# Three single-precision-part products in place of fp32 ones in the first mixer's branch and output projections

## What is computed

```python
def hybrid_mixer(x, w_in, b_gate, ..., w_branch_dn, w_branch_sb, w_out):
    proj = x @ w_in
    ...
    gate = jax.nn.sigmoid(gates.reshape(b, l, N_BRANCH, d) + b_gate)
    merged = (gate[:, :, 0] * (o_dn.astype(x.dtype) @ w_branch_dn)
              + gate[:, :, 1] * (o_sb.astype(x.dtype) @ w_branch_sb))
    return merged @ w_out
...
mix = hybrid_mixer(h, ...)
h = layer_norm(DEEPNORM_ALPHA * h + mix, ln1_g[i], ln1_b[i])
ffn = hierarchical_moe(h, ...)      # router, then 32 experts, top 2 of a group
```

## Time and profile before

| | |
|---|---|
| Time before | 1086.28 us, median of 3 runs (1086.09 to 1087.94) |
| Profiled execution | 1088.23 us, of which 1086.1 us lie between its first and last instruction (the span) |
| PE busy | 983.1 us, 91% of the span |
| VectorE, ScalarE, GpSimd busy | 498.5, 354.2 and 33.8 us |
| DMA | 229.38 MB, 211 GB/s over the span |
| Mean granted TensorE clock | 0.964 of 2.4 GHz |

### The profile page before, as it was taken

One profiled execution on the slowest core, in us unless ns is written; L12 is line 12 of the kernel. 1 busy time (PEld: TensorE's weight loads), 2 busy tenths in 40 slices (PEclk: granted clock), 3 DMA queues, 4 the chain that ended last, 5 costly groups with the idle time before them and its releaser, 6 DMA issues.

```text
span 1086.1 us, 14285 instructions
## 1 busy us (share of the span) xinstructions
PE 983.1 (91%) x6105; PEld 726.6 (67%) x6105; DVE 498.5 (46%) x777; ACT 354.2 (33%) x456; POOL 33.8 (3%) x51
## 2 busy tenths in 40 slices
PE   8989989999999984656877999999999989999996
PEld 7988776444456432213336887599998879889995
DVE  5973563271246102001038446355656565655554
ACT  3555303841022110001025436134343334434341
POOL 1400100021000000000000000000000000000000
PEclk9989999999999997878999999999999999999999
DMA  9724420452942999999995460445545344545520
GB/s 334 218 86 148 147 88 1 155 184 97 415 156 100 417 421 421 421 421 421 422 396 189 156 227 5 155 155 191 197 164 222 118 154 155 213 175 198 189 77 39
DMA packets 67126, 229.38 MB, mean 211 GB/s; under 512 B 4080, under 2 KB 5392, under 8 KB 54400
## 3 DMA queue, kind: packets, MB, share of 16 engines
q1 hardware_dynamic: 65216, 223.28, 54.2%
q0 software_dynamic: 1632, 5.26, 1.3%
q10 hardware_dynamic: 224, 0.07, 0.0%
HBM read 227.54 MB, written 1.05 MB: 210 GB/s over the span
## 4 chain that ended last, share of the span: by engine, by line
PE 74%; DMA 12%; DVE 9%; issue 2%; SPq 2%; ACT 1%; DVEq 0%; ACTq 0%
PE bank L1253 17%; PE bank L1264 16%; PE bank L1036 5%; DMA ring<-in_expert_w_up 5%; PE bank L676 4%; DMA arena<-in_expert_w_up 3%; PE bank L1162 3%; PE bank L665 3%; PE bank L960 3%; PE bank L929 3%; PE bank L1229 3%; PE bank L652 2%; DMA arena<-in_expert_w_down 2%; DVE arena L1744 2%; PE bank L1167 2%
## 5 line engine op out<-in xcount | busy, mean ns | idle before, releaser
L2174 DVE TENSOR_TENSOR w_lo<-ring,w_hi 128x2048 fp32r<-128x2048 f32 x76 | 170.6, 2288 | 97.4 <-ACT w_hi L1556 97.4
L1556 ACT ACTIVATE w_hi<-ring 128x2048 fp32r<-128x2048 f32 x76 | 141.1, 1909 | 87.9 <-PE bank L1264 86.9
L1253 PE MATMUL bank<-xT_hi,w_hi 128*128 128x256 f32 x512 | 143.8, 281 | 2.6 <-DVE xT_lo L2162 2.6
L1253 PE MATMUL bank<-xT_hi,w_lo 128*128 128x256 f32 x512 | 143.6, 280 | 0.0
L1253 PE MATMUL bank<-xT_lo,w_hi 128*128 128x256 f32 x512 | 143.2, 280 | 0.0
L1264 PE MATMUL bank<-w_hi,hidden_lo 128*128 128x512 f32 x256 | 99.9, 390 | 0.0
L1264 PE MATMUL bank<-w_lo,hidden_hi 128*128 128x512 f32 x256 | 99.8, 390 | 0.0
L1264 PE MATMUL bank<-w_hi,hidden_hi 128*128 128x512 f32 x256 | 99.6, 389 | 0.0
L1253 PEld LDWEIGHTS bank<-xT_hi,w_hi 128*128 128x128 f32 x512 | 96.1, 188 | 3.5 <-issue 3.0
L1253 PEld LDWEIGHTS bank<-xT_lo,w_hi 128*128 128x128 f32 x512 | 96.4, 188 | 0.5
L1253 PEld LDWEIGHTS bank<-xT_hi,w_lo 128*128 128x128 f32 x512 | 95.9, 187 | 0.0
(11 more groups left out here) (489 smaller groups left out, 1621.5 us busy)
## 6 DMA issues: line engine op xcount, KB each, us to landing
ring<-in_mlp_w_up SPq DMA_DIRECT2D x32, 1024.0 KB, 6.6
ring<-in_mlp_w_down SPq DMA_DIRECT2D x32, 1024.0 KB, 6.3
ring<-in_w_in SPq DMA_DIRECT2D x22, 1024.0 KB, 7.6
ring<-in_expert_w_down SPq DMA_DIRECT2D x22, 1024.0 KB, 19.7
ring<-in_expert_w_gate SPq DMA_DIRECT2D x16, 1024.0 KB, 15.4
ring<-in_expert_w_up SPq DMA_DIRECT2D x16, 1024.0 KB, 17.4
arena<-in_expert_w_gate SPq DMA_DIRECT2D x15, 1024.0 KB, 12.8
arena<-in_expert_w_up SPq DMA_DIRECT2D x15, 1024.0 KB, 14.8
```

Of the source, the lines that this page charges most:

```text
L1253: last = mm(B[4 + (2 * j + pr) % 4][:, cc * SEQ:(cc + 1) * SEQ], w_[:, k * 512 + c * P:k * 512 + (c + 1) * P], x_[:, k, 0:SEQ], start=(k = ...
L1556: act(whi[:, n % 2, half], slot(u)[:, half], ACT.Copy).then_inc(S("split_hi"), 1)
L2174: tt(wlo[:, u % SLOTS, half], slot(u)[:, half], f32(whi[:, n % 2, half]), ALU.subtract).then_inc(S("split_lo"), 1)
```

## The change

The two branch projections and the output projection are each made of three single passes. The four weight units are split by halves of 2048 columns (h = 0 to 7). ScalarE writes the hi part of a half to one of three buffers `mid_hi` (in X2, in `params` columns 2048 to 4095 and in `params` columns 0 to 2047), and VectorE writes the lo part over the half in its ring slot. `mid_split(h)` waits for the half to land and, from h = 3 on, for the products that read the buffer last (`HALF_FREE`). The left operands are split too: `od_hi`, `od_lo`, `os_hi`, `os_lo`, `xT_hi` and `mix_lo`. A bank is summed over both halves of a unit. Since `params` and X2 are in use longer, expert units 0 and 1 now wait for the end of the output projection. The constants `lower_r` and `ones_r` move from X2 to `arena`.

```diff
+    mid_hi = [parts("mid_hi0", "X2", 0, HALF_U), parts("mid_hi1", "params", 2 * D, HALF_U), parts("mid_hi2", "params", 0, HALF_U)]
...
-    FIRST_USE = [0, 5, 6, 7, 8, 2, 1, 3, 4]
+    FIRST_USE = [8, 5, 6, 7, 2, 3, 0, 1, 4]
...
+    HALF_FREE = ("half_used", 1), ("branch", 4), ("half_used", 2), ("branch", 8), ("half_used", 3)
...
-            elif j == 0:
-                sp.wait_ge(S("gate_out"), 8)
-                sp.wait_ge(S("stream_made"), 2)
-            elif j == 1:
-                sp.wait_ge(S("four_psum"), 4)
+            elif j < 2:
+                sp.wait_ge(S("mixed"), 4)
...
+        def branch(u, ready, hi, lo):
+
+            for part in range(2):
+                h = 2 * (u - 11) + part
+                weights_split(h, "split_hi")
+                passes = (hi, mid_hi[h % 3]), (lo, mid_hi[h % 3]), (hi, wlo[:, u % SLOTS, part * HALF_U:(part + 1) * HALF_U])
+                for p_, n in [(p_, n) for p_ in range(3) for n in range(4)] if part == 0 else [(p_, n) for n in range(4) for p_ in range(3)]:
...
+                    for kk in range(2):
+                        last = mm(B[n], x_(2 * part + kk, i), w_[:, kk * D + half * 512:kk * D + (half + 1) * 512], start=(part == 0 and p_ == 0 and kk == 0), stop=(part == 1 and p_ == 2 and kk == 1))
...
+        def mid_split(h):
+
+            u, half = 11 + h // 2, slice((h % 2) * HALF_U, (h % 2 + 1) * HALF_U)
+            landed(sc, u)
+            if h >= 3:
+                sc.wait_ge(S(HALF_FREE[h - 3][0]), HALF_FREE[h - 3][1])
+            act(mid_hi[h % 3], slot(u)[:, half], ACT.Copy).then_inc(S("split_hi"), 1)
...
+        def mid_low(h):
+
+            u, half = 11 + h // 2, slice((h % 2) * HALF_U, (h % 2 + 1) * HALF_U)
+            dve.wait_ge(S("split_hi"), MID0 + h + 1)
+            tt(wlo[:, u % SLOTS, half], slot(u)[:, half], f32(mid_hi[h % 3]), ALU.subtract).then_inc(S("split_lo"), 1)
+
+        for i in range(NT):
+            dve.wait_ge(S("branch_in"), i + 1)
+            tt(odL[:, 4 * i:4 * i + 4, :], cube(B[6 + i], 4), f32(odH[:, :, i * P:(i + 1) * P]), ALU.subtract).then_inc(S("branch_lo"), 1)
+        mid_low(0)
```

More of the change, by code:

```diff
@@ L223, in build @@
     SP0s, SP1s = (cube(SPH[0], 8), cube(SPL[:, 0:2048], 8)), (cube(SPH[1], 8), cube(SPL[:, 2048:3072], 8))
-    lower_r, ones_r = [parts(f"{n}_r", "X2", P * i, P) for i, n in enumerate(("lower", "ones"))]
+    lower_r, ones_r = [parts(f"{n}_r", "arena", 18240 + P * i, P) for i, n in enumerate(("lower", "ones"))]
+    mid_hi = [parts("mid_hi0", "X2", 0, HALF_U), parts("mid_hi1", "params", 2 * D, HALF_U), parts("mid_hi2", "params", 0, HALF_U)]
+    odH, odL = cube(parts("od_hi", "arena", 8 * L, 1024), 4), cube(parts("od_lo", "arena", 12 * L + 8 * L + 1536, 1024), 8)
+    osH, osL = cube(parts("os_hi", "arena", 4 * L, 1024), 4), cube(parts("os_lo", "arena", 12 * L, 1024), 4)
+    mixL = [cube(parts(f"mix_lo{i}", "X1", (2 * i + 1) * D, D), 4) for i in range(2)]
     wr, rbias = cube(arena[:, 18496:18496 + KD * 36], KD), arena[:, 18784:18820]
@@ L916, in _ @@
             last.then_inc(S("later_psum"), 1)
-        def branch(u, src, n, ready):
-            landed(pe, u)
-            pe.wait_ge(S("branch_in"), ready)
-            for i in range(NT):
-                for half in range(2):
-                    if n < 4:
-                        pe.wait_ge(S("later_out"), n + 1)
-                    else:
-                        pe.wait_ge(S("branch_out"), n - 3)
-                    for k in range(4):
-                        last = mm(B[n % 4], src[:, k, i * P:(i + 1) * P], slab(u, k, D)[:, half * 512:(half + 1) * 512], start=(k == 0), stop=(k == 3))
-                    last.then_inc(S("branch"), 1)
-                    n += 1
@@ L934, in _ @@
+        branch(11, 2, lambda k, i: odH[:, k, i * P:(i + 1) * P], lambda k, i: odL[:, 4 * i + k, :])
         pe.wait_ge(S("masked"), 4)
@@ L1916, in _, with gated @@
             tt(ZM[:, hs, :], ZM[:, hs, :], cube(B[(6, 7, 4, 5)[g]][0:META, :], 2), ALU.subtract).then_inc(S("later_out"), 1)
+        mid_low(1)
+        mid_low(2)
         dve.wait_ge(S("gate_sig"), 8)
-        for n in range(8):
+        def gated(n):
             br, i, half = n // 4, (n // 2) % 2, n % 2
@@ L1923, in _ @@
             tt(g_, g_, B[n % 4], ALU.mult).then_inc(S("branch_out"), 1)
+        for n in range(4):
+            gated(n)
+        mid_low(3)
+        for i in range(NT):
+            dve.wait_ge(S("branch_in"), i + 3)
+            tt(osL[:, 2 * i:2 * i + 2, :], cube(B[6 + i], 2), f32(osH[:, 2 * i:2 * i + 2, :]), ALU.subtract).then_inc(S("branch_lo"), 1)
+        mid_low(4)
+        for n in range(4, 8):
+            gated(n)
         for i in range(NT):
@@ L1926, in _ @@
             tt(gates[:, i, 0, :], gates[:, i, 0, :], gates[:, i, 1, :], ALU.add).then_inc(S("merged"), 1)
-        four_copies(0)
+        dve.wait_ge(S("merged"), 2)
+        for b in range(4):
+            dve.wait_ge(S("turned_act"), b + 1)
+            tt(mixL[b // 2][:, 2 * (b % 2):2 * (b % 2) + 2, :], cube(B[4 + b], 2), f32(xTH[:, 2 * b:2 * b + 2, 0:SEQ]), ALU.subtract).then_inc(S("turned_dve"), 1)
+        for h in range(5, MID):
+            mid_low(h)
         dve.wait_ge(S("stream_made"), 2)
```

79 lines of the change are left out of this document (60 added, 19 removed).

## The result

| | before | after |
|---|---|---|
| Median on one chip, in turns | 1088.12 us (1086.09 to 1089.28, 8 runs) | 1078.20 us (1077.27 to 1083.48, 8 runs) |
| Ratio | | 0.9922, 95% interval 0.9905 to 0.9939 |
| Profiled execution | 1088.23 us, span 1086.1 | 1078.01 us, span 1076.0 |

The change is faster by 8.5 us by the ratio (10.3 to 6.6) and by 9.9 us by the two medians. The ratio is the smaller one since two of the eight executions of after lie well above the rest (1081.62 and 1083.48 us); the means are 8.6 us apart. The sum said 10.3, the two profiled executions are 10.2 apart (spans 10.1).

The account below looks back on a forecast made before the run. PE was taken to bound the kernel (busy 983.1 of 1086.1 us), with the projections all on the path. Gains of 11.0 us less a 0.7 us wait gave -10.3 us: median 1076.0, own range 1074.0 to 1077.6, 8 in 10 1073.3 to 1079.2.

Parts of the forecast that it names:

- The sum: Whole kernel: -11.0 + 0.7 = -10.3 us; profiled execution to about 1077.9, median from 1086.28 to 1076.0.
- The passes: Branch and output projections: 192 single passes at 0.230 us (0.2275 to 0.233) replace 64 fp32 matmuls, gaining 11.0 us.
- the two prices: Projections: skill page's 215.7 ns per isolated matmul (sum 2.7 us better) or some 131 ns sustained (19 us better).
- The case with a price of 0.213 us a pass: Projections, rival "more than forecast": a pass costs only its 512 columns, 3.2 us more gain, 1072.8; chance 0.05.
- The wait of the third META group: Ahead of the first branch: PE waits for VectorE's delayed subtractions, 0.7 us lost, bounds nothing and 2.3.
- The half clock in front of the output projection: Output projection: 0.58 us at half clock, soon after PE's pause behind the second branch, was kept as staying.
- Splits: Branches and output projection: hi and lo halves ready in time, no PE stall, margins of 1.5 us and more.
- The rival of late splits: Projections: one or two halves late through VectorE's queue or GpSimd contention, 1 to 4.6 us, 1077.6 to 1081; chance 0.11.
- Expert loads: Units 0, 1 and 4, issued at about 303.9, land by about 319; products at 327.6, 8 us left, cost nothing.
- the rival's mechanism: Late expert units: transfers wait for each other or take far longer, cost 1 to 10 us, 1078 to 1086; chance 0.04.
- Carried to the end: Stages behind the projections have no clock of their own and shift by 10 us, unchanged in length; gain reaches the end whole.
- The median: Whole kernel: profiled execution 1.95 us above the median of 1086.28, a difference left outside the argument; new median 1076.0.

Follow-up runs that it names:

- e14: The kernel before, unaltered, profiled alone a fourth time; single time 1085.76 us.
- e15: The changed kernel, unaltered, profiled alone for a third profile; single time 1078.22 us.
- e9: The kernel before timed against itself, with a second profile of it; 1087.19 us, ratio 0.9999.
- e13: The kernel before, unaltered, profiled alone for a third profile; single time 1087.77 us.
- e5: The changed kernel unaltered, timed again against the kernel before; 1079.05 us, ratio 0.9930.
- e8: Changed kernel with the passes of each unit's second half ordered by k, so a hi left part's two products adjoin; against before 1078.28 us, ratio 0.9926.
- e6: Changed kernel with lo half 0 on VectorE moved behind the six subtractions; against before 1078.94 us, ratio 0.9921.
- e16: The changed kernel, unaltered, profiled alone for a fourth profile; single time 1081.54 us.
- e4: Changed kernel with expert units 0, 1 and 4 waiting for the second router product group; against before 1089.41 us, ratio 1.0014.
- e3: Changed kernel with two buffers for hi halves instead of three; against before 1079.49 us, ratio 0.9921.
- e12: Changed kernel with expert units 0, 1 and 4 waiting for the first router product group; against before 1081.97 us, ratio 0.995.
- e1: Changed kernel with the branches back in fp32, only the output projection in passes; against before 1084.97 us, ratio 0.997.
- e2: Changed kernel with the output projection back in fp32, only the branch projections in passes; against before 1084.38 us, ratio 0.9974.
- e7: Changed kernel with idle matmuls in four pauses of PE, from behind the second branch to the gather; against before 1077.90 us, ratio 0.9911.
- e10: Changed kernel with both e6's moved lo half 0 and e7's idle matmuls; against before 1076.70 us, ratio 0.9896.
- e11: e10 plus idle matmuls ahead of the last quad's expert and down products and the attention's first lo products; against before 1078.00 us, ratio 0.9908.

## Why the prediction was right in the stage, and which step failed

**The passes: right, and a little slower than said.** Where both kernels ran the stage at full clock, from the second META group to the end of the output projection, e14 took 284.02 + 27.72 - 240.43 = 71.31 us and e15 281.61 + 22.56 - 243.08 = 61.09: **-10.2 us**, forecast -10.3. The same stretch takes 71.31 us in e9 and 71.30 in e13, and 61.10 in after and in e5, so this number does not hang on the choice of the pair. The steps are 11.12/48 = 0.232, 11.37/48 = 0.237 and 22.55/96 = 0.235, where 0.230 was taken with 0.233 as the upper end. That is 45.04 us in place of 44.16, 0.9 too few. The 0.230 leaned on the MLP's 0.2275. In this stage even the middle of a stream has 0.2325 (e8), and two of the three stretches start behind a pause, which costs 0.24 us more each. Why the MLP's step is smaller no run here shows.

Of the two prices discussed there, the Trainium skill's page "TensorE: Matmul & The Clock Gate", section "Back-to-back issue gap", gives some 216 ns for isolated 512-column matmuls at full clock, an estimated 20.7 us for the 96 passes. The trace disagrees, with 22.55 here and 22.57 in e8 with the left operand repeated. The case with a price of 0.213 us a pass is out. (Its 0.05 is missing from the 0.13 that the prediction counted outside its range, since 1072.8 lies below 1073.3; 8 in 10 still fits.)

**The wait of the third META group: right in place and cause, too large.** 0.20 us, forecast 0.7. The chain names what was named, `od_lo`, lo half 0 and the first subtractions, and e6 removes it. The four subtractions (L1967) took 2.39 us on the chain where 2.7 had been laid out, and PE came to the second group 0.2 us later than in the row used, for reasons ahead of this place. The wait is thus 0.5 us below the forecast, which with the 0.3 us that the fp32 stage held above the row used (27.72 for the output projection at full clock against 27.46) makes up for most of the steps. The sum was right partly by luck, since its errors cancel.

**The half clock in front of the output projection: not kept.** The prediction carried 0.58 us over as something that belongs to the pause (and, without naming it, 0.87 more in transposes that "cost what they did"). It belongs to the execution. Either kernel has it in one profile (before, 28.04; e16, 23.40) and not in another (e14, 27.72; after, 22.55), with the same pause.

**Splits: right.** No PE idle ahead of a pass in after, but for the 0.74 us in front of the second branch that before has too; a lo half beside GpSimd (L585) was early as forecast; even two buffers cost 0.5 us. The rival of late splits is out.

**Expert loads: right.** Unit 1 landed at 315.7, slack of 12 us where 8 were forecast; the 8 counted the bytes of unit 4 too, which stands behind unit 1 in the queue and which the first products don't need. e4 shows the rival's mechanism when it is forced, 20 us of delay for 11 us of time.

**Carried to the end: right in the profile.** From the first expert products to the last down products (L1073 before, L1102 now) it is 212.79 us before and 212.90 in after, and behind it 535.35 and 535.47.

**The median: the step that failed.** It stands in "The sum": the profiled execution is 1.95 us above the median of 1086.28, "and the difference lies outside this argument". That median was of 3 executions. With the five that were then taken in turns with the changed kernel it came to 1088.12 us, 0.11 us below the profiled one, and the same kernel had 1087.47, 1087.76 and 1086.9 in the later comparisons (26, 11 and 19). So the profiled execution was no slow one, and the 1.95 us that the sum took off measured 0.11. Of the 2.2 us between 1076.0 and 1078.20, 1.8 are this term (1088.12 - 1086.28), and the other 0.4 are the gain itself, 9.9 us by the medians where 10.3 had been set. The profile's own forecast, "about 1077.9", met 1078.01.

**The clock's stretches: the assumption beneath it.** The sum was made between two executions with the stretches at half clock left where they were, and one profile stood for the usual execution. The ratios of 8.5 and 7.6 us (e5) are under the 10.2 of the stage. In the profiles the difference comes with the stretches, which lie elsewhere in each execution. The four profiles of each kernel are 336.73 and 328.24 us on average at the first expert products, -8.5; that this is the timed number to a tenth is luck with four of each, since without e16 it would be -9.4. Of the 1.7 us that are missing to 10.2, 1.2 lie ahead of the second META group (240.72 and 241.89 on average), where PE does the same in both kernels, and 0.8 are the stretch on the first branch that e16 alone has; behind the projections after is 0.25 us the better.

Two places come back in many profiles. At 160 to 164 us a stretch costs 1.3 us (the two matmul pairs of one line there take 1.54 and 1.65 us in e5, 0.86 and 1.05 in e6); at 278 to 284 it costs 1.4 in the changed kernel (e6: 0.66 on the transposes, 0.72 on the output projection) and 1.2 at 283 to 288 in before. Both in all profiles:

| | stretch at 160 | stretch at 278 to 288 | neither |
|---|---|---|---|
| before (4 profiles) | 1 | 1 (the same) | 3 |
| all projections in passes, no idle matmuls added (after, e3 to e6, e8, e12, e15, e16) | 5 | 5 (e12 has both) | 0 |
| only the output projection in passes (e1) | 1 | 1 (the same) | 0 |
| only the branches in passes (e2) | 0 | 0 | 1 |
| with idle matmuls added (e7, e10, e11) | 1 | 0 | 2 |

The profile that the prediction was made from is the one of before that had both; the three others had neither, and every one of the changed kernel had at least one. If that were the rule, the gain would be 10.2 less 1.3 or 1.4, 8.9 or 8.8, between the ratios' 8.5 and 7.6 and the medians' 9.9 and 8.7. But the execution with both took 1088.23 us, as much as the median of eight in the result (1088.12), so it isn't shown that the usual execution there had neither. e16, with the stretch on the first branch, shows what makes an execution of 1081.54 us. Behind the projection, up to the first expert products, the two kernels don't differ: 23.75 to 25.10 us before, 23.53 to 25.12 after, so the router and the gather, which I suspected at first, are not where the 2 us went.

The idle matmuls test this from the other side. None of the three kernels with them had the stretch at 278. The evidence is in e10 and e11, which had none at 160 either, where four of four changed kernels without them had it at 278; e7 had the one at 160, and with that four of five had none at 278 anyhow. e10 gains 11.3 us by its ratio (13.3 to 9.2) where the change alone has 8.5 and 7.6. That a microsecond is lost at the pause in front of the transposes is thereby supported by two profiles and intervals that overlap a little, no more.

What isn't shown is why. In the kernel before, the three profiles with none at 160 had none at 278 either, with the same pause of 1.92 us ahead of the transposes. The obvious candidate, passes in place of fp32 records ahead of the pause, has one run against it: e2 has the passes there, the same pause of 1.92 us and no stretch at 160, and its transposes took 1.09 us twice, at full clock. And 5 of 9 against 1 of 4 at 160 may be chance. So where the stretches fall, and with it the last 1 to 2 us between the stage's 10.2 and the ratios, stays open.

## What to carry over

Replacing an fp32 product by three single passes saved (0.858 - 3 x 0.235)/0.858 = 18% of its PE time here, as long as each half of a weight is split while the half before it multiplies. When the gain is a per cent, time the kernel before more than three times and take several profiles of it: here the median of the first three was 1.8 us below that of all eight, which was most of the miss, and a stretch at half clock on a row of the chain is a property of that execution; which executions are the usual ones is not to be seen in one. And when a faster stage leaves PE's pauses where they were, a few idle matmuls in the pauses ahead of it and behind it are worth a try: here the ratios came out 1 to 4 us better, with intervals that overlap, and six runs lay within 2.0 to 3.5 us, where e5 had 6.0 and e6 4.0. Further ones later in the run did nothing.

## What the runs showed of the hardware

- The same kernel ran at 1.2 GHz at other places in each execution. In its four profiles, between 100 and 330 us, the changed kernel did so at 161 and 321 (after), 160 and 314 (e5), 161 and 315 (e15), and at 243, 281 and 315 us (e16). A stretch cost 1.0 to 1.7 us where it met the path (last down products 5.37 us in e5, 3.67 in after), the long one at 243 to 251 us in e16 some 3 us. Differences of a third of a per cent between two runs are thereby nothing that an edit has to explain.
- Where GpSimd and VectorE worked side by side, the one that started later took longer. L584 took 2.00 us, its twin L585 took 4.11. It started 0.03 us behind a lo half, which took 2.27 us, as other lo halves do (2.20 to 2.43):

```profile
246.31 2.00 POOL L584 TENSOR_TENSOR arena<-arena,cst 128x1024 f32<-128x1024 f32 x1 [22.14 <-ACT arena L1519]
248.26 4.11 POOL L585 TENSOR_TENSOR arena<-arena,cst 128x1024 f32<-128x1024 f32 x1
```

```profile
248.23 2.27 DVE L1958 TENSOR_TENSOR w_lo<-ring,mid_hi 128x2048 fp32r<-128x2048 f32 x1
```

  L585 ends 1.87 us behind the lo half's end. In the earlier trace rows L580 took 2.97 us against 1.99 and L1904 2.91 against 1.23: L580 ends 1.87 us behind L1903, which had started first (220.11 + 2.02), and L1904, which started during L580, ends 1.07 us behind it. In all three it looks as if the later one waited for the end of the earlier; no run here tests that by itself. The prediction had both in line at worst.
- 24 passes take 5.58 us in the middle of a stream and 5.82 at its start behind a pause, at full clock (e8).
